# A two-layer hybrid trunk on one core: the gated recurrence in two visits to PE instead of four, and an opening with statistics by quarters

## What is computed

```python
bcum = cumsum(logf)                                # decay, summed along the chunk
diff = bcum[t] - bcum[s]                           # for each pair s <= t and each channel
attn[t, s] = sum_d q[t, d] * k[s, d] * exp(diff[t, s, d])
o = attn @ v + (q * exp(bcum)) @ state
state = exp(bcum[-1]) * state + (k * exp(bcum[-1] - bcum)).T @ v
```

## Time and profile before

| | |
|---|---|
| median of 3 runs | 1025.55 us (1025.49 to 1025.58) |
| the profiled execution, its own time | 1027.41 us |
| its span, first to last instruction | 1025.6 us |
| mean granted clock of TensorE | 0.997 |
| PE matmuls busy | 1013.7 us, 99% |
| DVE, ACT, POOL busy | 642.7, 517.2, 287.4 us |
| HBM | 91 GB/s over the span |
| instructions | 15346 |

### The profile page before, as it was taken

One profiled execution on the slowest core, in us unless ns is written; L12 is line 12 of the kernel. 1 busy time (PEld: TensorE's weight loads), 2 busy tenths in 40 slices (PEclk: granted clock), 3 DMA queues, 4 the chain that ended last, 5 costly groups with the idle time before them and its releaser, 6 DMA issues.

```text
span 1025.6 us, 15346 instructions
## 1 busy us (share of the span) xinstructions
PE 1013.7 (99%) x6406; PEld 855.2 (83%) x6406; DVE 642.7 (63%) x840; ACT 517.2 (50%) x804; POOL 287.4 (28%) x144
## 2 busy tenths in 40 slices
PE   8999999999999999999999999999999999999997
PEld 7878999788888888888888989988888888888876
DVE  6978965899444443536638689479973444444552
ACT  6866665865633222323366766567546323232333
POOL 1122114324332323324112111153243232322430
PEclk9999999999999999999999999999999999999999
DMA  7532122122232323325243222212232232322602
GB/s 222 153 103 64 63 83 83 42 83 83 62 103 83 103 82 103 99 68 162 83 134 103 67 79 84 83 49 77 83 103 62 82 103 84 101 89 96 204 2 82
DMA packets 93428, 94.71 MB, mean 92 GB/s; under 512 B 2272, under 2 KB 91568, under 8 KB 93360
## 3 DMA queue, kind: packets, MB, share of 16 engines
q1 hardware_dynamic: 93232, 93.70, 29.8%
q10 hardware_dynamic: 128, 0.04, 0.0%
HBM read 91.64 MB, written 2.10 MB: 91 GB/s over the span
## 4 chain that ended last, share of the span: by engine, by line
PE 92%; DVE 5%; ACT 1%; issue 1%; DMA 1%; SPq 0%; DVEq 0%; ACTq 0%
PE pj L512 27%; PE pj L513 26%; PE pj L514 26%; PE mx L649 2%; PE mx L512 1%; PE mx L513 1%; PE mx L514 1%; PE mx L612 1%; PE mx L709 1%; PE mx L677 1%; PE mx L597 1%; PE mx L687 1%; PE mx L589 1%; DMA x_tokens<-in_x 1%; DVE rope_cos L1427 1%
## 5 line engine op out<-in xcount | busy, mean ns | idle before, releaser
L1168 POOL TENSOR_TENSOR w_lo<-w_raw,w_hi 128x1024 fp32r<-128x1024 f32 (+1 forms) x89 | 195.9, 2201 | 566.5 <-ACT w_hi L825 566.3
L512 PE MATMUL pj<-h_hi,w_hi 128*128 128x512 f32 x832 | 329.7, 396 | 0.4 <-DVE w_lo L1278 0.4
L514 PE MATMUL pj<-h_hi,w_lo 128*128 128x512 f32 x832 | 324.2, 390 | 0.0
L513 PE MATMUL pj<-h_lo,w_hi 128*128 128x512 f32 x832 | 324.1, 389 | 0.0
L825 ACT ACTIVATE w_hi<-w_raw 128x1024 fp32r<-128x1024 f32 (+1 forms) x179 | 159.1, 938 | 160.3 <-PE pj L514 160.1
L1278 DVE TENSOR_TENSOR w_lo<-w_raw,w_hi 128x1024 fp32r<-128x1024 f32 (+1 forms) x90 | 159.9, 1777 | 67.9 <-ACT w_hi L825 67.7
L512 PEld LDWEIGHTS pj<-h_hi,w_hi 128*128 128x128 f32 x832 | 156.2, 188 | 34.8 <-issue 3.2
L514 PEld LDWEIGHTS pj<-h_hi,w_lo 128*128 128x128 f32 x832 | 156.2, 188 | 33.1
L513 PEld LDWEIGHTS pj<-h_lo,w_hi 128*128 128x128 f32 x832 | 156.3, 188 | 31.9 <-issue 1.0
L1392 DVE TENSOR_TENSOR merge_gate<-pj,rstd 128x512 f32<-128x512 f32 x48 | 33.2, 692 | 162.9 <-PE pj L514 162.9
L943 ACT ACTIVATE merge_gate<-merge_gate,small 128x512 f32<-128x512 f32 x48 | 34.3, 715 | 89.3 <-DVE merge_gate L1392 89.3
(11 more groups left out here) (259 smaller groups left out, 1502.0 us busy)
## 6 DMA issues: line engine op xcount, KB each, us to landing
w_raw<-in_w_in SPq DMA_DIRECT2D x61, 1024.0 KB, 5.5
w_raw<-in_w_branch SPq DMA_DIRECT2D x24, 512.0 KB, 3.4
w_raw<-in_w_out SPq DMA_DIRECT2D x6, 1024.0 KB, 5.2
x_tokens<-in_x SPq DMA_DIRECT2D x4, 512.0 KB, 7.3
w_raw_last<-in_w_out SPq DMA_DIRECT2D x2, 1024.0 KB, 8.1
sp_w_rows<-in_sp_w SPq DMA_DIRECT2D x2, 512.0 KB, 6.3
out<-out_low SPq DMA_DIRECT2D x4, 256.0 KB, 2.0
out<-out_high SPq DMA_DIRECT2D x4, 256.0 KB, 2.3
```

The lines of the kernel that those rows point to most:

```text
L512: pe.matmul(bank, wh, ah, start=first, stop=False)
L513: pe.matmul(bank, wh, al, start=False, stop=False)
L514: return pe.matmul(bank, wl, ah, start=False, stop=final)
L1168: return pool.tensor_tensor(out=dst, in0=full, in1=hi.bitcast(f32), op=ALU.subtract)
```

## The change

1. Levels go from 7 to 5 (s = 64 to 4). What is left are blocks of four positions: `diagonal` now multiplies `key_blocks` by `query_blocks`, k and q each scaled by the exponential of half the distance to the middle of their block (`block4_diffs`, `block4_exp`, `block4_operands`), and `take_block4` clears `attnT` and copies under a mask.
2. A table `STEPS` places every step. PE does the first product with levels 0 and 1 in hook 13 (28 for p = 1) and levels 2, 3 and 4 in hook 17 (32). Each half of a PSUM bank holds a level; level 4 writes into `key_blocks`. The second half's k_hat steps move from hooks 34 to 37 to 35 to 38.
3. In DVE's phases the calls of the recurrence other than clamp, sums and `block4` come behind `normalise`.
4. The gate products of cg's jobs 36 and 37 and their high and low parts move to phase 40; in a phase with a gate product DVE's half of the weights' low part goes ahead of it. POOL waits in phase 34 until the levels are done.
5. Opening: transposes 2 and 3 move behind the matmuls of k = 0; bn_stats come in 16 calls of 256 columns, a quarter of x at a time; ACT's and DVE's split of unit 1 move up; `bounds` and its exponential move from phases 7 and 6 to phase 2.

```diff
-LEVELS = 7
-DIAG = (12, 25)
-PAIRS = ((0,), (1, 2), (3, 4), (5, 6))
+LEVELS = 5
+STEPS = (dict(block_diffs4=10, block_exp4=10, block_ops=11, first_exps=12, first_ops=13, first=13, second_exps=14,
+              first_taken=14, second_ops=15, last_exp=16, last_ops=17, second=17, second_taken=18, carry_exp=19,
+              decayed=20, khat=21),
+         dict(block_diffs4=24, block_exp4=25, block_ops=26, first_exps=27, first_ops=28, first=28, second_exps=29,
+              first_taken=29, second_ops=30, last_exp=31, last_ops=32, second=32, second_taken=33, carry_exp=34,
+              decayed=35, khat=35))
...
+        HK = [at(f"key_blocks{p}", [P, 2 * T], r) for p, r in enumerate((r_brh + 16 * KB, r_brl + 12 * KB))]
+        HQ = [at(f"query_blocks{p}", [P, 2 * T], r) for p, r in enumerate((r_sg, r_scr + 12 * KB))]
...
+        def level_ops(p, lev):
+            return HK[p] if lev == LEVELS - 1 else XL[lev % 2]
+
+        def level_bank(lev):
+
+            return (M[3][:, 0:T // 2], M[3][:, T // 2:T], M[4][:, 0:T // 2], M[4][:, T // 2:T], M[3][:, 0:T // 2])[lev]
...
-            transpose_x(2)
-            transpose_x(3)
...
-                            if k in (2, 3):
+                            if k in (1, 2, 3):
...
                 def diagonal(p):
-                    evacuated(pe, FIRST[("cq", p)] + 1, layer)
-                    pe.wait_ge(c_keys, upto(c_keys, p + 1))
+                    pe.wait_ge(ops_ready, upto(ops_ready, (LEVELS + 1) * p + 1))
...
+                            b = slice(hb * P + half * 64, hb * P + half * 64 + 64)
+                            last = pe.matmul(M[4][rows, hb * 64:(hb + 1) * 64], HK[p][:, b], HQ[p][:, b],
...
-                for p, d in enumerate(DIAG):
-                    hooks[d + 1].append((diagonal, p))
-                    for i, levels in enumerate(PAIRS):
-                        for lev in levels:
-                            hooks[d + 1 + 2 * i].append((level, p, lev))
+                for p, at_ in enumerate(STEPS):
+                    hooks[at_["first"]].append((diagonal, p))
+                    for lev in (0, 1):
+                        hooks[at_["first"]].append((level, p, lev))
+                    for lev in (2, 3, 4):
+                        hooks[at_["second"]].append((level, p, lev))
                     for step, f in enumerate((transpose_khat, state_updates, recurrent_out, head_norm)):
-                        hooks[d + 2 + LEVELS + step].append((f, p))
+                        hooks[at_["khat"] + step].append((f, p))
...
+            split_hi(1)
             x_evac(5)
             x_evac(2)
             x_evac(3)
-            split_hi(1)
...
+                def block4_exp(p):
+                    act.wait_ge(diff_done, upto(diff_done, (LEVELS + 2) * p + 1))
+                    act.activation(E[1][:, :], E[0][:, :], ACT.Exp, scale=0.5)
+                    act.activation(E[0][:, :], E[0][:, :], ACT.Exp, scale=-0.5).then_inc(decay_ready, 1)
...
                     phase[2].append((rstd_row,))
+                    phase[2].append((bounds_exp,))
                     phase[2].append((first_sines,))
-                    phase[6].append((bounds_exp,))
...
+                    phase[at_["block_exp4"]].append((block4_exp, p))
+                    for lev, when in enumerate(("first_exps", "first_exps", "second_exps", "second_exps", "last_exp")):
+                        phase[at_[when]].append((decay_exp, p, lev))
+                    phase[at_["carry_exp"]].append((block_exp, p))
+                    phase[at_["khat"] + 1].append((khatT_out, p))
+                    phase[at_["khat"] + 3].append((recurrent_evac, p))
+                    phase[at_["khat"] + 4].append((head_rstd, p))
...
+                    if kind == "bg" and ct == 2:
+                        pool.wait_ge(lev_done, upto(lev_done, 2 * (LEVELS + 1)))
...
-            def x_stats(half, tb):
-                return dve.bn_stats(XS[:, tb, half, :], XTOK[:, tb, half * T:(half + 1) * T])
+            def x_stats(j):
+                dve.wait_ge(x_in[j], 16)
+                for tb in range(TB):
+                    last = dve.bn_stats(XS[:, tb, j, :], XTOK[:, tb, 2 * j * P:2 * (j + 1) * P])
+                return last
...
+            x_stats(0)
             first_low(2)
             quarter(1)
             first_low(3)
-            dve.wait_ge(x_in[0], 16)
-            dve.wait_ge(x_in[1], 16)
-            x_stats(0, 0)
-            x_stats(0, 1)
+            x_stats(1)
             split_half(0, 1)
             first_low(4)
             first_low(5)
-            x_stats(0, 2)
-            x_stats(0, 3)
+            x_stats(2)
             first_low(6)
             first_low(7)
-            dve.wait_ge(x_in[2], 16)
-            dve.wait_ge(x_in[3], 16)
-            for tb in range(TB):
-                last = x_stats(1, tb)
-            pchain(last)
+            split_lo(1)
+            pchain(x_stats(3))
             for tb in range(TB):
                 last = dve.bn_aggr(MV[:, tb, :], XS[:, tb, :, :])
             pchain(last)
             pchain(dve.tensor_tensor(out=MS, in0=MV[:, :, 0], in1=MV[:, :, 0], op=ALU.mult))
             dve.tensor_tensor(out=MS, in0=MS, in1=MV[:, :, 1], op=ALU.add).then_inc(p_ms, 1)
-            split_lo(1)
...
+                def block4_diffs(p):
+
+                    if p == 0:
+                        dve.wait_ge(rope_done, upto(rope_done, 5))
+                    else:
+                        dve.wait_ge(state_ready, upto(state_ready, 1))
+                    b = BC[p][:, :, :].rearrange("p h t -> p (h t)").rearrange("p (b u) -> p b u", u=4)
+                    mid2 = E[1][:, 0:2 * T // 4]
+                    chained(dve.tensor_tensor(out=mid2, in0=b[:, :, 1], in1=b[:, :, 2], op=ALU.add))
+                    dve.scalar_tensor_tensor(out=E[0][:, :].rearrange("p (b u) -> p b u", u=4), in0=b, scalar=2.0,
+                                             in1=mid2.unsqueeze(2).to_broadcast([P, 2 * T // 4, 4]),
+                                             op0=ALU.mult, op1=ALU.subtract).then_inc(diff_done, 1)
...
+                def block4_operands(p):
+                    dve.wait_ge(decay_ready, upto(decay_ready, (LEVELS + 2) * p + 1))
+                    if p == 1:
+                        dve.wait_ge(oc_done, upto(oc_done, 1))
+                    dve.tensor_tensor(out=HK[p][:, :], in0=KK[p][:, :, :].rearrange("p h t -> p (h t)"),
+                                      in1=E[0][:, :], op=ALU.mult)
+                    evacuated(dve, FIRST[("cq", p)] + 1, layer)
+                    dve.tensor_tensor(out=HQ[p][:, :], in0=QC[p][:, :, :].rearrange("p h t -> p (h t)"),
+                                      in1=E[1][:, :], op=ALU.mult).then_inc(ops_ready, 1)
...
+                    dve.wait_ge(decay_ready, upto(decay_ready, (LEVELS + 2) * p + lev + 2))
+                    back = (0, 0, 2, 3, 1)[lev]
+                    if p + back > 0:
+                        dve.wait_ge(lev_done, upto(lev_done, (LEVELS + 1) * p + back))
+                    e, o = halves(E[lev % 2][:, :], s), halves(level_ops(p, lev)[:, :], s)
...
-                    dve.memset(at4[64:128, :, 0:64], 0.0)
+                    chained(dve.memset(AT[:, :, :], 0.0))
                     for half in range(2):
                         rows = slice(half * 64, half * 64 + 64)
-                        last = dve.tensor_tensor(out=at4[rows, :, half * 64:half * 64 + 64],
-                                                 in0=M[4][rows, :].rearrange("p (b t) -> p b t", t=64),
-                                                 in1=ID[rows, rows].unsqueeze(1).to_broadcast([64, 2 * TB, 64]),
-                                                 op=ALU.mult)
+                        last = dve.copy_predicated(at4[rows, :, half * 64:half * 64 + 64],
+                                                   MASK4[rows, :].unsqueeze(1).to_broadcast([64, 2 * TB, 64]),
+                                                   M[4][rows, :].rearrange("p (b t) -> p b t", t=64))
...
-                    dve.wait_ge(lev_done, upto(lev_done, (LEVELS + 1) * p + lev + 2))
+                    dve.wait_ge(lev_done, upto(lev_done, (LEVELS + 1) * p + (3, 3, 5, 5, 6)[lev]))
...
+                    phase[2].append((bounds,))
                     phase[2].append((trig,))
-                    phase[7].append((bounds,))
...
+                    phase[at_["block_diffs4"]].append((block4_diffs, p))
+                    phase[at_["block_ops"]].append((block4_operands, p))
+
+                def recurrence_rest(p):
+                    at_ = STEPS[p]
+                    for lev in (0, 1):
+                        phase[at_["block_ops"]].append((diffs, p, lev))
+                    for lev in (0, 1):
+                        phase[at_["first_ops"]].append((operands, p, lev))
+                    for lev in (2, 3):
+                        phase[at_["first_ops"]].append((diffs, p, lev))
```

(27 more changed lines are left out.)

106 lines of the change are left out of this document (35 added, 71 removed).

## The result

The changed kernel takes 1034.54 us, median of four runs (1033.92 to 1037.49), beside 1025.57 for the kernel before (1025.49 to 1025.72): a ratio of 1.0093, with a 95% interval of 1.0073 to 1.0113. It is slower by 9.0 us. The prediction said slower, 3.3 us, and its range ended at 1033.0: the sign was right, the size was not, and the value lies outside the range. The profiled execution took 1034.94 us.

A forecast was written before the change was run, and what follows sets the result against it. The prediction took the length of PE's queue as the bound. Its terms, -8.2 - 0.9 + 9.6 + 2.8 = +3.3 us, gave a median of 1028.9 us, range 1017.9 to 1033.

The forecast's parts named there:

- PE's queue: PE's level matmuls in the recurrences: two of six levels and two visits go, 2.05 us per recurrence, -8.2 us.
- opening, up to job 10: First jobs through rope: PE starts earlier and the wait before job 10 goes, net -0.9 us, between -2.0 and +0.6.
- wait before level 4: Hook 17: PE waits 4.8 us per layer for level 4's products, queued on DVE behind neg_max(3) and normalise(3), +9.6 us.
- clock behind it: Behind the wait before level 4: PE's clock is halved, costing 1.4 us per layer, +2.8 us, ends 0 and 2.8.
- first meeting: DVE between scores(2) and neg_max(3): its SBUF work stands still beside POOL's split of unit 9, 2.2 us.
- second meeting: Level 4's second product on DVE starts at 32.4, stands until 34.5 beside POOL's split of unit 10, ends at 35.1.
- Start 0.2: DVE after scores(2): it begins neg_max(2) 0.2 us behind the end of those scores.
- sign against itself: DVE's phase 15: a scan at 2.6 us there would show the forecast wrong.
- their exponential falls into a wait of ACT: Opening: the exponential of the moved bounds runs while ACT waits, with one table load more, 1.28 us.
- wait without clock loss: Rival at level 4: the wait comes but the clock stays full, +0.5 us, 1026.1; chance 0.25.
- third rival: Layer 0: DVE falls further behind and unit 8's low half is late for job 16, up to 2.6 us, 1031.5; chance 0.15.
- slow take_block4: DVE's block copy, untraced, taken at 2.55 us; a slower one with the third rival sets the range's end, 1033.

The follow-up runs named there:

- experiment 12: The kernel before, unchanged, profiled once more: 1025.48 us in one execution.
- experiment 5: The changed kernel with level 4's products ahead of normalise(3) and the low half of unit 8 ahead of take_block4 on DVE: 1017.92 us, ratio 0.9921.
- experiment 3: The changed kernel with level 4's products moved between neg_max(3) and normalise(3) in DVE's phase 17: 1019.27 us, ratio 0.9938.
- experiment 4: The changed kernel with POOL's split of unit 10 held until level 4's products are done: 1030.82 us, ratio 1.0048.
- experiment 6: The changed kernel with POOL's split of unit 9 held until neg_max(3), that of unit 10 until level 4's products: 1025.19 us, ratio 0.9992.
- experiment 8: The kernel of experiment 5 with transposes 2 and 3 put back ahead of the first jobs: 1015.82 us, ratio 0.9905.
- experiment 13: The kernel before with the new opening, but transposes 2 and 3 left ahead of the first jobs: 1025.03 us, ratio 0.9996.
- experiment 1: The kernel before with only the opening of the change, transposes 2 and 3 moved behind k = 0 included: 1027.20 us, ratio 1.0012.
- experiment 2: The changed kernel with the old opening put back: 1034.60 us, ratio 1.0091.

## Why the prediction was right and where it failed

The balance of the change against the second profile of before, in us: predicted, then measured by the traces.

| term | predicted | measured | from |
|---|---|---|---|
| PE's queue | -8.2 | -9.1 | traces: -2.1 per first half, -2.4 and -2.5 per second |
| opening, up to job 10 | -0.9 | +1.1 | 71.34 in experiment 12, 72.41 after |
| wait before level 4 | +9.6 | +10.7 | first row of waits |
| clock behind it | +2.8 | +5.0 | 2.1 and 2.9 |
| wait before job 16 | 0 | +1.6 | experiment 5 |
| sum | +3.3 | +9.3 | medians +9.0, profiled 1034.94 - 1025.48 = 9.5 |

Four terms missed. By size they are the clock (2.2 us), the opening (2.0), job 16 (1.6) and the wait itself (1.1); PE's queue gave back 0.9.

**The wait: right in kind and nearly in size.** The sentence "PE waits 35.1 - 30.3 = 4.8 us" came out in layer 1 by the way that it describes: scores(2) end at 605.02, DVE begins neg_max(2) 0.35 behind them, the first meeting falls on the scan (4.80 instead of 2.62, the predicted 2.2), the second on the last product, which ends at 640.77. That is 35.75 instead of 35.1, and PE wanted it at 30.3. It was 5.5. In layer 0 the 5.2 is made of other parts. "Start 0.2" failed there: DVE began neg_max(2) at 102.69, 2.4 us behind scores(2), still busy with the products and differences of phase 13. The first meeting was cheaper, 1.5 instead of 2.2, since it fell on the two keys and left the scan at 2.62, which the prediction had named as a sign against itself and which held in this layer only. And PE itself came 1.6 later, by job 16. Experiments 3, 4 and 6 settle the cause: with the call elsewhere the wait is 0, without the second meeting 3.1 to 3.3, without both 1.2 to 1.6 (the prediction had 2.9 with one meeting and 0.7 with none).

**Step that failed first: the opening, "Net -0.9, between -2.0 and +0.6".** It was read from the earlier trace rows, an execution in which a late piece of x made PE idle for 2.26 us and halved its clock. Against that execution it is right: job 10 starts at 73.31 there and at 72.41 after. The prediction saw that the profiled execution was 1.9 above the median and carried this over as a constant to both kernels. It lay in the very stretch that the change edits. In the usual execution PE stands 1.25 or less there at full clock, and the new opening makes it stand 1.85 for DVE's quarter, with the clock halved behind it in every trace that has this opening. The transposes were meant to fill idle time, and moved they leave PE with nothing to do while it waits (experiments 8 and 13 against 5 and 1: 2.1 and 2.2 us). Bounds and statistics cost nothing that shows in the time. Moved out of phase 7, bounds do save the wait of 1.1 before job 10, and job 6 now waits about as much for unit 3's low half. And "their exponential falls into a wait of ACT" is only half of it: the table loaded for bounds before served softmax_exp(0) too, and now that one loads its own, 1.28 us between neg_max(0) and normalise(0). What this costs by itself was not tried.

```profile
64.25 1.28 ACT L971 ACT_TABLE_LOAD   x1 [2.54 <-DVE small L1478]
```

**Second: the clock, "I charge 1.4 in each layer: +2.8, with ends 0 and 2.8".** The opening's price was taken for the price of any wait, and its double for the upper end. Behind the waits of 3.1 to 5.5 us it was 2.1 to 3.0, because level 4 and the front of job 18 both ran at 1.2 GHz. 1.4 is nearest to the short waits of experiment 6 (1.7). The rival "wait without clock loss" fell: in no trace did PE wait before level 4 for 1.2 us or more with the clock kept. The Trainium skill (TensorE: Matmul & The Clock Gate, Part 1) says that the clock is given by activity; the rows agree.

**Third: job 16.** The prediction's third rival had the place and the price, "the low half of unit 8 ... up to 2.6 more", and I gave it 0.15 beside the forecast instead of adding it. Its reason, "DVE comes out of rope 1.5 us later", is right in that DVE is late in layer 0, 2.4 us at neg_max(2) against 0.35 in layer 1, where the same queue makes no wait. As a cost of the new opening it is wrong: with the old one DVE was 3.0 behind and the wait longer (experiment 2). The wait takes both, DVE's lateness in layer 0 and the place of the split in phase 14, behind take_block4 and two levels; one call moved took it away (experiment 5). Where the lateness comes from was not taken apart. take_block4 itself was 2.5, as estimated.

**Right:** the records from 768 to 512; 2.05 us per recurrence for the first halves, a little more for the second; statistics at 0.35 apiece; rope's end at 59.1 (58.9); the second meeting (2.83 against 0.68). The end of the range went by the third rival and a slow take_block4. The clock at its measured size would have carried the forecast to 1031, and job 16 on top of it to 1033; the opening made the rest.

Open: the changed kernel's four runs spread over 3.6 us, those of before over 0.2. The halved clock after level 4 differed between the layers of one trace by 0.8 us, so it may be that, and the runs speak for it: the slowest, 1037.49, has the lowest mean granted clock, 0.987 beside 0.988 to 0.990. Experiment 2 with the same wait spreads over 3.2 us in the same way, and experiment 3 without it over 0.8. No trace of a slow one was taken.

## What to carry to other kernels

When calls are gathered into fewer visits, list for each what now stands ahead of it in every engine's queue, and put each product that PE waits for into a gap where that engine stands anyway: here one line moved was 15 us. Before a stretch is costed from one trace, look at whether that execution is the usual one, and if it lies off the median, look for the difference inside the stretch that is edited. Charge a wait on PE of a microsecond or more with its length and, at the upper end, with the halved clock behind it, here 1.2 to 3.0 us each.

## What the runs showed of the hardware

In the traces, whether the clock fell did not go by the length of the wait alone. Between jobs of 512 columns PE waited 2.02 us and kept 2.4 GHz, while 2.81 was followed by 1.2 GHz. Directly behind three levels of 32-column matmuls 2.03 was, before level 4, with two levels ahead of it and one behind, 1.2, and before job 16, behind eight transposes of 128 columns, 2.06, where 1.41 was not. These are single executions, and the same kernel does not always do the same: one of eleven in experiment 1 took 1025.20 us where the others took 1026.60 or more, and one of four in experiment 5 took 1015.92 (mean clock 0.999) where the others took 1017.90 to 1017.97 (0.997). That the matmuls around the wait decide is thus a guess that fits; it isn't shown.

Where the clock fell, what it cost did not grow with the wait: between 1.2 and 3.0 us beyond the length, 1.2 behind a wait of 2.03, 2.9 behind 3.1 and 3.3, 1.6 behind 6.98. It went by how long PE still ran at 1.2 GHz behind the end of the wait: 4.4, 6.2 and 3.3 us there cost 2.1, 2.9 and 1.6.

The prediction took it that DVE stands still beside POOL where both inputs are in SBUF. The keys of L1502 read one tile and a column of scalars, and they took 2.50 instead of 1.00 beside POOL's split at 116.02. The Trainium skill (GPSIMD Engine Reference, section 8, Key points) names DVE's 2-port modes next to the two inputs; the row agrees with that wider rule as far as it goes, since no view shows the mode. The held one can be POOL, too: its split that starts at 99.52, while DVE runs four differences one behind the other at their usual 0.68 us, takes 4.82 us instead of 2.4.
